# A hybrid decoder step on eight cores: reordered statistics in load_norm, both cross-attention cache loads of the samples on one queue with two buffers each

## The reference, cut to what matters

```python
def rmsnorm(x, g):
    xf = x.astype(jnp.float32)
    y = xf * lax.rsqrt(jnp.mean(xf * xf, axis=-1, keepdims=True) + EPS) * g.astype(jnp.float32)
    return y.astype(x.dtype)

def cross_attn(h, mk, mv, w):
    B, T, _ = h.shape
    q = (h @ w['w_cq']).reshape(B, T, X_HEADS, X_HD)
    s = jnp.einsum('bthd,bnhd->bhtn', q, mk.astype(q.dtype)).astype(jnp.float32) * (X_HD ** -0.5)
    p = jax.nn.softmax(s, axis=-1)
    o = jnp.einsum('bhtn,bnhd->bthd', p.astype(h.dtype), mv.astype(h.dtype)).reshape(B, T, D_MODEL)
    return o @ w['w_co']

def block(x, ..., mk, mv, w):
    y, new = mixer(rmsnorm(x, w['g_mix']), ...)          # RG-LRU group and mLSTM group
    x = x + y
    x = x + cross_attn(rmsnorm(x, w['g_xattn']), mk, mv, w)
    hf = rmsnorm(x, w['g_ffn'])
    x = x + jnp.square(jax.nn.relu(hf @ w['w_up'])) @ w['w_down']
```

## Time and profile before

| | us |
|---|---|
| median of the three runs shown | 4375.99 |
| the three runs | 4224.83, 4375.99, 4431.43 |
| the profiled execution | 4241.95 |
| its span, slowest core (core 6) | 4240.4 |
| spans of all cores | 4202.0 to 4240.4 |
| load_norm of `xp`, of `xm`, of the memory | 54.8, 54.7, 19.2 |
| the samples' cross-attention | 402 |

### The profile page before, as it was taken

The page is one execution under the profiler, slowest core; times in us unless marked ns, Lnnn a source line. Parts: engine busy times, 40 slices in busy tenths (PEclk is TensorE's granted clock), DMA queues, the critical chain, the costliest instruction groups (busy, mean ns, idle before and its releaser), DMA issues.

```text
span 4240.4 us, 43355 instructions; the slowest of 8 cores (4202.0 to 4240.4 us)
## 1 busy us (share of the span) xinstructions
PE 2638.6 (62%) x15142; PEld 1296.9 (31%) x15142; DVE 1115.7 (26%) x2459; ACT 835.6 (20%) x1536; POOL 282.8 (7%) x325
## 2 busy tenths in 40 slices
PE   2244317754267383653458595444859999999983
PEld 0121113221033131221334242333424444444432
DVE  0043451222331303133215404222132121222224
ACT  0011111124423333233120211111021010100113
POOL 1012300000000000000001000111000000000000
PEclk8555558777578595776689896555879999999996
DMA  8813334110143020400767343666535565655612
GB/s 111 117 54 119 108 121 69 31 21 0 50 80 50 1 40 1 70 15 5 124 155 90 39 61 70 127 125 131 76 39 72 70 71 75 74 71 71 77 23 81
DMA packets 339204, 295.12 MB, mean 70 GB/s; under 512 B 14556, under 2 KB 316380, under 8 KB 334384
## 3 DMA queue, kind: packets, MB, share of 16 engines
q0 software_dynamic: 279568, 182.04, 33.2%
q1 hardware_dynamic: 59424, 110.32, 7.9%
HBM read 443.26 MB, written 31.10 MB: 112 GB/s over the span
## 4 chain that ended last, share of the span: by engine, by line
PE 52%; DMA 18%; DVE 14%; ACT 8%; issue 7%; DVEq 1%; ACTq 0%; SPq 0%; POOLq 0%; POOL 0%
PE ps L359 50%; DMA arena<-cv 8%; ACT arena L353 6%; DMA arena<-s_C 3%; DMA arena<-w_in 3%; PE ps L362 2%; DVE arena L768 2%; ACT L353 1%; DVE arena L762 1%; DVE arena L1348 1%; DMA arena<-w_mv 1%; DMA arena<-w_mk 1%; DVE arena L1093 1%; DVE arena L1000 1%; DVE arena L502 1%
## 5 line engine op out<-in xcount | busy, mean ns | idle before, releaser
L359 PE MATMUL ps<-arena 128*128 128x512 bf16 (+7 forms) x13846 | 2409.0, 328 | 1150.0 <-ACT arena L353 329.7
L359 PEld LDWEIGHTS ps<-arena 128*128 128x128 bf16 (+3 forms) x13846 | 1108.6, 103 | 2463.3 <-issue 1506.5
L353 ACT ACTIVATE arena<-ps 128x512 bf16<-128x512 f32 (+9 forms) x879 | 401.3, 470 | 2342.6 <-PE ps L359 1726.7
L362 PE MATMUL ps<-arena 128*128 128x128 f32 (+5 forms) x1296 | 238.9, 359 | 447.6 <-DVE arena L494 118.2
L362 PEld LDWEIGHTS ps<-arena 128*128 128x128 f32 (+5 forms) x1296 | 192.7, 188 | 475.6 <-issue 472.9
L353 ACT ACTIVATE arena<-arena 128x512 bf16<-128x512 f32 (+9 forms) x329 | 212.8, 653 | 589.5 <-DVE arena L1233 142.2
L1310 DVE TENSOR_TENSOR arena<-arena 128x512 bf16<-128x512 f32 (+1 forms) x192 | 94.1, 518 | 379.5 <-ACT arena L353 379.5
L1317 DVE TENSOR_TENSOR arena<-arena,ps 128x512 f32<-128x512 f32 (+1 forms) x192 | 93.4, 513 | 371.3 <-PE ps L359 371.3
L353 ACT ACTIVATE arena<-ps,arena 128x512 f32<-128x512 f32 (+4 forms) x200 | 120.0, 602 | 264.8 <-PE ps L359 257.6
L353 ACT ACT_TABLE_LOAD x77 | 98.8, 1283 | 204.5 <-PE ps L359 88.6
L150 POOL DMA_DIRECT2D arena<-w_in x29 | 33.2, 1145 | 1332.9 <-PE ps L359 706.7
(11 more groups left out here) (158 smaller groups left out, 705.2 us busy)
## 6 DMA issues: line engine op xcount, KB each, us to landing
arena<-w_in POOLq DMA_DIRECT2D x26, 2048.0 KB, 16.1
arena<-ck SPq DMA_DIRECT2D x64, 512.0 KB, 5.2
arena<-w_up POOLq DMA_DIRECT2D x32, 1024.0 KB, 11.1
arena<-w_down POOLq DMA_DIRECT2D x32, 1024.0 KB, 9.1
arena<-s_C SPq DMA_DIRECT2D x16, 1024.0 KB, 8.2
o_sC<-arena SPq DMA_DIRECT2D x16, 1024.0 KB, 5.4
arena<-xm SPq DMA_DIRECT2D x16, 1024.0 KB, 5.7
arena<-cv POOLq DMA_DIRECT2D x64, 256.0 KB, 4.9
```

The source lines that it names most:

```text
L353: k.op("act", lambda e: e.activation(out, in_, func, **kw), reads=reads, writes=writes)
L359: k.op("pe", lambda e: e.matmul(out, lhsT, rhs, start=start, stop=stop), reads=reads, writes=writes, inc=inc)
L362: k.op("pe", lambda e: e.transpose(out, in_, ident), reads=reads, writes=writes, inc=inc)
```

## The change

Two places. In `load_norm` the chunk's work is cut in two: `stage_a` is the DMA, the sum of squares and the three small steps up to the reciprocal, `stage_b` is the scaling, the transposes and the gain. Stage a of chunk i+1 is emitted ahead of stage b of chunk i. The buffers stay as they were, two of each.

```diff
+            ng = T // 128
+
+            def stage_a(i):
                 s2 = i % 2
                 k.dma("sp", stg[s2], src[i * 128:(i + 1) * 128, :], writes=[stgb[s2]])
                 act(junk, stg[s2], AF.Square, [stgb[s2]], [junkb, stb], accum_out=st[:, 0:1])
...
                 dve(lambda e, st=st: e.reciprocal(st[:, 3:4], st[:, 2:3]), [stb], [stb])
+
+            def stage_b(i):
...
                 dve(lambda e, s2=s2, xb=xb, st=st: e.tensor_scalar(xb, stg[s2], st[:, 3:4], None, op0=ALU.mult), [stb, stgb[s2]], [xbb])
...
+            stage_a(0)
+            for i in range(ng):
+                if i + 1 < ng:
+                    stage_a(i + 1)
+                stage_b(i)
```

```diff
-            Ks = [A.alloc([2, 512], F32) for _ in range(2)]
-            mkTs = A.alloc([4, 256], BF16)
-            mvts = A.alloc([2, 512], BF16)
+            Ks = [A.alloc([2, 512], BF16) for _ in range(2)]
+            mkTs = [A.alloc([4, 256], BF16) for _ in range(2)]
+            mvts = [A.alloc([2, 512], BF16) for _ in range(2)]
...
-                    k.dma("sp", Ks[s2], ck_d[tok][:, hd * 512:(hd + 1) * 512].rearrange("(nh p) d -> p nh d", p=128), writes=[b_Ks[s2]])
-                    k.dma("pool", mvts, cv_d[tok][:, hd * 512:(hd + 1) * 512].rearrange("(nh p) d -> p nh d", p=128), writes=[b_mv1])
...
+            def st_a(it):
+                tok, hd = its[it]
+                s2 = it % 2
+                k.dma("pool", Ks[s2], ck_d[tok][:, hd * 512:(hd + 1) * 512].rearrange("(nh p) d -> p nh d", p=128), writes=[b_Ks[s2]])
+                k.dma("pool", mvts[s2], cv_d[tok][:, hd * 512:(hd + 1) * 512].rearrange("(nh p) d -> p nh d", p=128), writes=[b_mv1[s2]])
+                b = tr_bank()
+                pv = psb(b)
+                for dc in range(4):
+                    for nh in range(2):
+                        tr(pv[:, (dc * 2 + nh) * 128:(dc * 2 + nh + 1) * 128], Ks[s2][:, nh, dc * 128:(dc + 1) * 128], idb, [b_Ks[s2], b_const], [pbuf[b]],
+                           inc=(dc == 3 and nh == 1))
+                if it % 2 == 0:
+                    act(mkTs[s2], pv.rearrange("p (c n) -> p c n", c=4), AF.Copy, [pbuf[b]], [b_mk1[s2]])
+                else:
+                    dv(lambda e, pv=pv, s2=s2: e.tensor_copy(mkTs[s2], pv.rearrange("p (c n) -> p c n", c=4)), [pbuf[b]], [b_mk1[s2]])
...
+            st_a(0)
+            for it in range(len(its)):
+                if it + 1 < len(its):
+                    st_a(it + 1)
+                st_b(it)
```

More of the change, by code:

```diff
@@ L485, in load_norm @@
             stg, stgb, xb2, xbb2, junk2, junkb2, st2, stb2 = scratch
-            for i in range(T // 128):
+            ng = T // 128
+            def stage_a(i):
                 s2 = i % 2
-                xb, xbb, junk, junkb, st, stb = xb2[s2], xbb2[s2], junk2[s2], junkb2[s2], st2[s2], stb2[s2]
+                junk, junkb, st, stb = junk2[s2], junkb2[s2], st2[s2], stb2[s2]
                 k.dma("sp", stg[s2], src[i * 128:(i + 1) * 128, :], writes=[stgb[s2]])
@@ L493, in load_norm @@
                 dve(lambda e, st=st: e.reciprocal(st[:, 3:4], st[:, 2:3]), [stb], [stb])
+            def stage_b(i):
+                s2 = i % 2
+                xb, xbb, st, stb = xb2[s2], xbb2[s2], st2[s2], stb2[s2]
                 dve(lambda e, s2=s2, xb=xb, st=st: e.tensor_scalar(xb, stg[s2], st[:, 3:4], None, op0=ALU.mult), [stb, stgb[s2]], [xbb])
@@ L1374, in attn_sample @@
             mk_ = A.mark()
-            Ks = [A.alloc([2, 512], F32) for _ in range(2)]
-            mkTs = A.alloc([4, 256], BF16)
-            mvts = A.alloc([2, 512], BF16)
-            ET = A.alloc([2, 16], BF16)
-            rden = A.alloc([16], F32)
-            b_Ks = [Buf("Ks0"), Buf("Ks1")]
[L1381 to L1386, removed]
-                    k.dma("sp", Ks[s2], ck_d[tok][:, hd * 512:(hd + 1) * 512].rearrange("(nh p) d -> p nh d", p=128), writes=[b_Ks[s2]])
-                    k.dma("pool", mvts, cv_d[tok][:, hd * 512:(hd + 1) * 512].rearrange("(nh p) d -> p nh d", p=128), writes=[b_mv1])
[L1389 to L1403, removed]
@@ new lines, in attn_sample @@
+            Ks = [A.alloc([2, 512], BF16) for _ in range(2)]
+            mkTs = [A.alloc([4, 256], BF16) for _ in range(2)]
+            mvts = [A.alloc([2, 512], BF16) for _ in range(2)]
+            ET = [A.alloc([2, 16], BF16) for _ in range(2)]
+            rden = [A.alloc([16], F32) for _ in range(2)]
+            b_Ks = [Buf("Ks0"), Buf("Ks1")]
+            b_mk1 = [Buf("mk0"), Buf("mk1")]
+            b_mv1 = [Buf("mv0"), Buf("mv1")]
+            b_ET = [Buf("ET0"), Buf("ET1")]
+            b_rden = [Buf("rd0"), Buf("rd1")]
@@ new lines, in attn_sample @@
+            its = [(tok, hd) for tok in range(NS) for hd in range(4)]
+            def st_a(it):
[13 more added lines that the diff above has]
+                    dv(lambda e, pv=pv, s2=s2: e.tensor_copy(mkTs[s2], pv.rearrange("p (c n) -> p c n", c=4)), [pbuf[b]], [b_mk1[s2]])
@@ new lines, in st_b @@
+            def st_b(it):
+                tok, hd = its[it]
+                s2 = it % 2
+                attn_core(1, [hd],
+                          lambda hd_, dc, nh: mkTs[s2][:, dc, nh * 128:(nh + 1) * 128], lambda hd_, dc: b_mk1[s2],
+                          lambda hd_, dc, nh: mvts[s2][:, nh, dc * 128:(dc + 1) * 128], lambda hd_, dc, nh: b_mv1[s2],
+                          qc_[:, :, tok:tok + 1], qcb_, oT_[:, :, tok:tok + 1], oTb_, ET[s2], b_ET[s2], rden[s2], b_rden[s2])
+            st_a(0)
```

## The result

The changed kernel is slower by 0.4%: a ratio of 1.004 to before, 95% interval 1.0024 to 1.0057, which is about 17 us. The profiled execution took 4252.75 us against 4241.95. The forecast was 4236, 6 us down, so the size is inside the range and the sign is wrong. Both halves of the sum were smaller than I had them, and the gain was out by more than the loss. In some executions the cores of one die show a lower clock and the time is some per cent longer: all ratios here compare executions without this, and of e5, which has none, only cores 4 to 7 are read.

A forecast was written before the change was run, and what follows sets the result against it. No engine fills the span; waits inside load_norm and the samples' attention (a loop over V's single buffer) go straight into it. From 4241.95 us, +56 for load_norm and -62 for attention gave 4236 us, range 4180 to 4300.

The forecast's parts named there:

- Both halves of the sum: Forecast change in span: load_norm +56 us, the samples' attention -62 us.
- The bound before: Samples' attention: one loop over V's single buffer, 6.28 us per iteration, with V's landing 5.07 of it.
- load_norm, the order: load_norm: the load joins DVE's loop, first scaling +2.7 us, last chunk -0.8; +56 us over three calls.
- load_norm keeps its pace: Rival: 1 MB loads land within the gains, 3.8 us after the scaling, so load_norm loses nothing; 4180 us, chance 0.05.
- the turn: load_norm's time per chunk in the new order: 9.9 us for xp, 10.3 for xm, where it was 5.90.
- The samples' attention, the mechanism: One loop spans two iterations, K queued behind V on POOL; 10.6 us for two, 5.31 each, -62 us.
- the slower copy sets both loops: Samples' attention: two loops, one per copy engine, alternate on PE; ACT's slower tail of 2.4 us sets both.
- L: Samples' attention: time from start of V's issue until K is there; 6.6 us taken, bounds 4.95 and 7.5.
- K early: Rival: K lands 4.95 us after V's issue starts, as if both ran side by side; 4183 us, chance 0.12.
- the wait only changes its name: Rival: PE waits as long for K as for V, an iteration stays 6.28 us; 4298 us, chance 0.07.
- The serial queue: Rival: K is served only after V has fully landed, 9.8 us, 6.9 per iteration; 4338 us, chance 0.06.
- the objection: load_norm, against the double-buffer rule: two tiles hid the load before; the new order takes the second tile's lead away.

The follow-up runs named there:

- e5: e4 with its loads taken from w_in in place of the caches; with full engines, 133 and 134 GB/s for e5 and e4 on core 5.
- e12: The kernel before, with each K or V load reading 512 KB in one piece; ratio 0.9898, 43 us less.
- e1: The kernel before with only the new load_norm, attention old; ratio 1.0094, 40 us more.
- e7: The kernel before with the new load_norm order and three staging tiles in place of two, attention old; ratio 1.0001.
- e2: The kernel before with only the new samples' attention, load_norm old; ratio 0.9955, 19 us less.
- e9: e2 with each load reading the same cache tensors as 512 KB in one piece; ratio 0.981 to the kernel before, 81 us less.
- e3: e2 with K loaded in f32 by SP into two tiles of its own, off V's queue; ratio 0.9723 to the kernel before, 118 us less.
- e4: e2 with K of iteration it+3 issued behind the transposes of it+1, all loads on POOL; ratio 0.9711 to the kernel before, 123 us less.

## Why the prediction was right or wrong

**The bound before** was read rightly for what it was, the slowest core's. It was a loop over V's single buffer: the chain names V at each turn, and in e12, where V lands 0.7 us earlier, the issues of V lie 0.8 closer over the eight cores and the time follows. (K lands earlier there too, but it had time to spare.) But the 6.28 us per iteration is core 6's. On core 1 of the same execution the 64 issues of V lie closer:

```profile
L150 POOL DMA_DIRECT2D arena<-cv x64: 696/702/717, 2579.0 to 2953.9; - x64
```

that is 374.9/63 = 5.95; over the eight cores it is 6.08. In e1 and e7, whose attention is the old one, it is 6.09 and 5.96 over the eight cores, 6.17 and 6.12 on the slowest. So 6.28 was the high end of one execution, and the gain per iteration had to be counted from about 6.08: 0.2 x 64 = 13 us of the 62 were never there. The changed kernel has 5.78 over its eight cores, 0.3 less or 19 us in all, as e2 measured, though e2's own profiled execution has 5.91.

**load_norm, the order** was right step by step: the load stands in DVE's turn, the first scaling is late by the second square, the last chunk saves a little. e7 shows that the lead of the load is the cause. The rival that load_norm keeps its pace fell. The size was +56 by the sum, +45 in the profile (+21.7, +21.3, +1.8), +40 in e1 (its interval reaches 46). The term that failed is the turn, 9.1 for 9.9. From the end of a scaling to the square took 5.0 to 5.1 us in five of the six turns (6.2 in the other) where I had 5.6 (and 6.0 for `xm`): I took medians of a stretch with a load every 5.9 us. With one every 9.1 the median landing of `xp` fell from 5.3 to 4.8; over the eight cores it is 4.8 to 5.3, and was 4.9 to 6.2. The trip from accumulator to scaling is 0.76, not 0.99, since the semaphore wait between reciprocal and scaling is gone.

**The samples' attention, the mechanism** was right: one loop over two iterations, POOL's V ahead of K. That the slower copy sets both loops is borne out only by the sum, which fits with the slower tail for this kernel and for e9; no run tried it alone. Its small terms came within 0.1: transposes 1.01 for 0.95, the tail 2.3 behind ACT's copy and 1.5 behind DVE's. The term that failed is **L**, 7.6 for 6.6, just past the upper end of its own range (7.5). Put into the sum it gives (0.53 + 7.6 + 0.14 + 1.01 + 2.3)/2 = 5.8, and the profile has 5.84 from the third V (2646.27) to the last (3002.5) in 61 steps. One us of L is 32 us of time; with the 13 above that covers the missing 43 (62 forecast, 19 in e2).

Where L failed is the choice between rows. I took V's landing of the old order, 4.9, and K's 256 packets at the `w_in` rate, 1.7. In the changed kernel V itself takes 5.6: the landing of one load is no constant. It grew when K's loads joined V's queue and the loads came closer together; in e3, where K is not on its queue, V takes 6.6, so the queue alone is not the reason, and which share is the traffic's was not tried. K adds 2.0 behind it; 128 to 137 packets per us, the rate of e4 with full engines, are 1.9 to 2.0 for 256. The first stage's 150 per us is not reached even by loads out of `w_in` itself (136 in e5), so it was the wrong row; why that stage is faster is not shown. A nearer one was in the trace of before: the software queue while the `w_mv` blocks stream (2090:2160), whose rows lie 8 KB apart as the caches' do:

```profile
q0 software_dynamic: 9443, 9.60, 104.3%
```

9443 packets in 70 us are 135 per us, 1.9 for 256. With that row L is 6.8 and the forecast 6 us higher, at no change. On the odd cores the same window has only 110 to 118 per us, which would have made L 7.1 to 7.2.

The Trainium skill (DMA: Bandwidth & Descriptors, Latency and other measured facts) gives rates for HBM row pitches of 512 KiB to 8 MiB, for copies between HBM tensors in tiles of 16 KiB per partition; it has none for a small pitch and no landing time. Here rows of 2 KB that lie 8 KB apart land in 6.3 us where one piece lands in 4.4 (V, e2 and e9). The same page's 2.0 us plus bytes at 436 GB/s (Anatomy of one DMA), an estimate of 3.9 with the issue, is nearer to the 4.4 of e9 and the 4.2 of e12 than to the 4.9 of before: the trace agrees with it best where the read is in one piece.

**The rivals.** K early (4183) fell. That the wait only changes its name (4298) was nearer than I gave it: PE's longest wait did become K, and the longer L took about half of the forecast gain (32 of 62 us). The serial queue fell, 7.6 and not 9.8. On the double-buffer rule of the Trainium skill (Trainium Kernel Development and Optimization, Best Practices) the runs agree with the objection: two tiles in the new order leave the load on every turn, three take it off (e7).

**The verdict on the sign.** The sum was a difference of two terms of some 60 us each with bounds of 30 us and more; its sign was not a finding, and I gave 0.90 to "within 2%", which held. That the total missed by only 23 us (6 down, 17 up) is luck: the loss was forecast 16 us too large and the gain 43 too large, and the two errors partly cancelled.

## What to carry to other kernels

Moving a wait ahead in program order is only free if the buffer it waits for is free by then: count the tiles that the new order has in flight, not those that it names "double". A load that is queued behind one that waits for a buffer inherits that wait; issue it where its own buffer comes free, and its latency matters much less (e2 to e4, 104 us for moved loads). And when a difference of two large terms decides the sign, take each duration from the row of the same tensor layout, and from all cores, not the slowest.

## What the hardware showed that I had not expected

- Rows of 2 KB that lie 8 KB apart in HBM make a single 512 KB load land 1.9 to 2.5 us later than one piece (e2, e9). A source whose single loads land sooner need not be faster with the engines full: `w_in` and the caches both gave 133 to 134 GB/s (e5, e4). Reads in one piece were not run with the engines full.
- The 1 MB loads of `xp` land in 4.8 us at the median with one every 9.1 us, in 5.3 with one every 5.9 (4.8 to 5.3 and 4.9 to 6.2 over the eight cores); the cause was not tried.
- DVE's copy of 128x1024 bf16 out of PSUM took 0.69 us, no more than its cast of 128x512 f32 did; L508, a multiplication of the same size, takes 1.23.
